# Declaring four ring slots of weights free together, behind the last value product of the mixing stage

## The reference, cut to what matters

```
xr, xw, xk, xv, xa, xg = [x + xx * mu[n] for n in range(6)]      # xx = x of the token before - x
r, k, v = xr @ w_rkv[0], xk @ w_rkv[1], xv @ w_rkv[2]            # 1024 x 1024 each
...
for each token t:                                                # state: 64 x 64 for each of 16 heads
    state = state * w_t + (state @ -kk_t) (kk_t * a_t) + v_t k_t
    y_t = state @ r_t
y = normalise(y) by head, times lnx_w, plus lnx_b, plus a bonus term times v
h = h + (y * g) @ w_o
```

## Time and profile before

| | |
|---|---|
| timed runs, us | 1700.23, 1700.84, 1712.27 (median 1700.84) |
| the profiled execution, us | 1709.79 |
| its span, first to last instruction, us | 1708.0 |
| mean granted TensorE clock | 0.988 of full speed |
| TensorE busy | 1667.2 us (98%) |
| the chain that ended last | TensorE 91%, VectorE 5%, DMA 2%, ScalarE 1% |

### The profile page before, as it was taken

How to read it: one execution, slowest core, us unless ns; L and a number is a source line. 1 busy time by engine, 2 the same in 40 slices (tenths; PEclk the granted TensorE clock), 3 DMA queues, 4 the chain that set the end, 5 groups by cost and what they waited for, 6 DMA issues and landing times.

```text
span 1708.0 us, 30174 instructions
## 1 busy us (share of the span) xinstructions
PE 1667.2 (98%) x12836; PEld 1297.3 (76%) x12836; DVE 906.1 (53%) x1926; ACT 699.5 (41%) x1348; POOL 5.0 (0%) x6
## 2 busy tenths in 40 slices
PE   9999999999999999999999999999989999999996
PEld 8889999787699699999887986555546798655553
DVE  6667565644467465657658765222126876523213
ACT  5576444432343354446548553111123655311111
POOL 0000000000000000000000000000000000000000
PEclk9999999999999999999999999999999999999998
DMA  8613353423200544525551455999992355599995
GB/s 338 246 70 146 156 221 125 169 99 148 88 3 4 221 184 162 214 108 197 195 187 38 175 194 217 426 424 424 425 423 82 110 196 198 218 427 426 422 426 225
DMA packets 36443, 373.80 MB, mean 219 GB/s; under 512 B 7232, under 2 KB 8384, under 8 KB 11728
## 3 DMA queue, kind: packets, MB, share of 16 engines
q1 hardware_dynamic: 33216, 366.18, 53.7%
q10 hardware_dynamic: 3088, 5.61, 1.0%
HBM read 370.73 MB, written 1.05 MB: 218 GB/s over the span
## 4 chain that ended last, share of the span: by engine, by line
PE 91%; DVE 5%; DMA 2%; ACT 1%; issue 1%; DVEq 0%; SPq 0%; ACTq 0%
PE ps L655 41%; PE ps L2346 12%; PE ps L2369 6%; PE ps L879 3%; PE ps L995 2%; PE ps L1526 2%; PE ps L2358 2%; PE ps L976 2%; PE ps L1770 2%; PE ps L2332 2%; PE ps L1739 2%; DMA ring<-in_w_moe 1%; PE ps L987 1%; PE ps L432 1%; PE ps L2834 1%; PE ps L2400 1%
## 5 line engine op out<-in xcount | busy, mean ns | idle before, releaser
L655 PE MATMUL ps<-ffn_x_h,ffn_w 128*128 128x256 f32 x1408 | 257.4, 283 | 0.2
L2346 PE MATMUL ps<-ring,expert_inputs 128*64 128x256 f32 x2048 | 235.1, 382 | 1.2 <-DMA ring<-in_w_moe 1.2
L655 PEld LDWEIGHTS ps<-ffn_x_h,ffn_w 128*128 128x128 f32 x1408 | 221.3, 192 | 1.5 <-DVE ffn_x_l L494 0.5
L647 ACT CAST w_h<-ring 128x512 fp32r<-128x512 f32 x240 | 149.3, 624 | 138.1 <-PE ps L655 130.0
L655 PE MATMUL ps<-ffn_x_l,ffn_w 128*128 128x256 f32 x704 | 199.2, 283 | 0.0
L650 DVE TENSOR_TENSOR w_l<-ring,w_h 128x512 fp32r<-128x512 f32 x240 | 164.1, 689 | 66.0 <-ACT w_h L647 62.0
L2346 PEld LDWEIGHTS ps<-ring,expert_inputs 128*64 128x64 f32 x2048 | 141.4, 137 | 70.4 <-DMA ring<-in_w_moe 1.3
L650 DVE TENSOR_TENSOR ffn_w<-ring,ffn_w 128x1024 fp32r<-128x1024 f32 x132 | 155.8, 1221 | 20.8 <-ACT ffn_w L647 20.8
L655 PE MATMUL ps<-w_h,x_h 128*128 128x512 f32 x384 | 150.1, 391 | 0.0
L655 PE MATMUL ps<-w_h,x_l 128*128 128x512 f32 x384 | 149.5, 389 | 0.0
L655 PE MATMUL ps<-w_l,x_h 128*128 128x512 f32 x384 | 149.4, 389 | 0.0
(11 more groups left out here) (374 smaller groups left out, 2674.6 us busy)
## 6 DMA issues: line engine op xcount, KB each, us to landing
ring<-in_w_moe SPq DMA_DIRECT2D x64, 2048.0 KB, 14.8
ring<-in_w_proj SPq DMA_DIRECT2D x37, 2048.0 KB, 8.0
ring<-in_w_ffn SPq DMA_DIRECT2D x22, 3072.0 KB, 10.2
ring<-in_w_moe SPq DMA_DIRECT2D x64, 1024.0 KB, 15.6
ring<-in_w_b_in SPq DMA_DIRECT2D x1, 2496.0 KB, 18.9
ring<-in_w_lora SPq DMA_DIRECT2D x1, 2048.0 KB, 8.1
rows<-in_ln_g SPq DMA_DIRECT2D x4, 512.0 KB, 3.6
rows<-in_ln_b SPq DMA_DIRECT2D x4, 512.0 KB, 5.1
```

The lines of the kernel that those rows point to most:

```text
L647: act.copy(high, x).then_inc(ready.up(), 1)
L655: last = pe.matmul(out, a[x], b[y], start=start and n == 0, stop=stop and n == 2, skip_group_check=True)
L2346: last = pe.matmul(bank(0)[g * SLOTS_E:(g + 1) * SLOTS_E, 0:2 * P], x[:, k, e * SLOTS_E:(e + 1) * SLOTS_E], wg[:, g, k, :], start=(k == 0) ...
```

## The change

Two lines are added behind the product of W6 on TensorE's list. `unit_done` issues nothing: it writes down, while the program is built, which semaphore value frees a slot. It is called a second time for W3, W4, W5 and W6 and overwrites what the calls inside `by_features` and `by_tokens` had set for them, one product at a time. The value is now that of the last product of W6, for all four.

```diff
                     last.then_inc(bonus_mm.up(), 1)
                     by_tokens(6, "v", V_OUT + 2)
+                    for i in range(3, 7):
+                        unit_done(j0 + i, mm)
                 stream(block, 6)
```

## The result

The changed kernel takes 1712.11 us (median of 20 runs, 1706.71 to 1722.24), the kernel before 1702.58 us (20 runs, 1699.62 to 1712.27). The ratio is 1.0055, with a 95% interval of 1.0041 to 1.0068: 9.4 us slower, 7.0 to 11.6. That is under the 1% that was named as the limit for a single comparison, but with this many runs it is clear of zero, and it is several times the 1.4 us that were forecast.

What follows compares the result with a forecast made beforehand. TensorE was taken to bound the kernel, with no transfer on the chain at the change. The only term, +1.4 us for VectorE's wait on the late lnx copies, added to the median gave 1702.2 us, range 1699.0 to 1709.0.

Steps and rivals of the forecast that it cites:

- What bounds the kernel: Whole kernel: TensorE busy 98% of the span, 91% of the chain; DMA 2%, no transfer on the chain at the change.
- what is moved: SP's loads wait for the end of W6's product: W7 later by 59.6 us, W8 by 42.4, W9 by 22.
- W7 to W9 themselves: The three loads in the scan: in by 485.2, first read at 552.01, 67 us of cover, so no cost.
- the products: Products ahead of the scan: loads leaving that stretch gain nothing, TensorE already busy throughout at clock 1.00; gain 0.
- What stands behind them in SP's queue: Four lnx copies queued behind W9: now behind 7 MB instead of 3, landing late for VectorE; the only cost seen.
- the sum: All terms together: +1.4 us with nothing against it, giving a median of 1702.2 us.
- The landing of the copies: Early scan: last lnx copy lands at 480.5 to 482.0, taken as 481.2.
- the wait that was priced at 1.4 us: First chunk: VectorE's copy of R starts at 481.2, but TensorE needs it by 479.8; cost 1.4 us, 0.7 to 2.2.
- The third rival: Scan: instruction fetches by DMA share engines with 7 MB; four fetches delayed 0.9 us each, 3.6 us, 1704.4; chance 0.05.
- The second rival: Around 482: the wait lowers TensorE's clock, +1.4 us; with slower loads, +2.8 to +8.2 us together; chance 0.15 including slower queue.
- The range: Median time of the changed kernel: 1699.0 to 1709.0 us, to hold the hidden case and most slower cases.
- The profile as a test: Signs of error: copies landing under 479.8, copies overtaking the loads, or granted clock 0.50 anywhere between 477 and 487.

Runs made afterwards that it cites:

- e8: Kernel before plus 6 MB of extra traffic beside the receptance and value products, where TensorE runs long matmuls; ratio 0.9994.
- e1: Changed kernel, but the four lnx copies issued ahead of W7, during the receptance products; ratio 1.0036 to the kernel before.
- e7: Kernel before, with only the four lnx copies (0.5 MB) held until the last value product; ratio 1.0003.
- e5: Kernel before, with W7, W8, W9 loaded a second time behind the last value product, 7 MB of extra traffic; ratio 1.0038.
- e3: Changed kernel, but W7, W8, W9 loaded in pieces of 4 KB per partition, all queued at once; ratio 1.0037 to the kernel before.
- e9: Changed kernel with lnx copies early and W7 to W9 in 0.5 MB pieces, each issued after the last landed; ratio 1.0002 to the kernel before.
- e11: Changed kernel with lnx copies early and W7 to W9 in 1 MB pieces, each issued after the last landed; ratio 1.0008 to the kernel before.
- e4: Changed kernel with lnx copies early and W7, W8, W9 issued 25 us apart in the scan; ratio 1.0043 to the kernel before.
- e6: Kernel before, with W7, W8, W9 loaded twice more behind the last value product, 14 MB of extra traffic; ratio 1.0072.
- e12: Changed kernel with lnx copies early and W7, W8, W9 as whole loads, each issued after the last landed; ratio 1.0037 to the kernel before.

## Why the prediction was wrong

**What bounds the kernel, what is moved, W7 to W9 themselves, the products**: right. TensorE carries the chain (92%), no load stands on it, W7 to W9 are in long before their use, and the products gained nothing by losing the loads (e8 adds some there without a loss).

**What stands behind them in SP's queue: "This is the one cost I see."** This is the step that failed, twice over: the cost was not there, and another, which the sum held at nothing ("+1.4 us, with nothing against it"), was. The landing of the copies was worked out to 0.3 us (24.3 forecast, 24.0 measured), from rows of queued loads. But the moment at which they are needed was taken from the trace of before, as if TensorE's work ahead of it stood fast under the new traffic. It didn't: the gaps and the low clock brought VectorE to its copy at 478.64 - 450.52 = 28.1 us into the scan, instead of 20.0. So the wait that was priced at 1.4 us was worth nothing: e1 takes it away and gains nothing at equal clock, e7 has the copies in the scan alone and loses nothing. In its place traffic alone costs 4.9 us at equal clock (e5), where the change costs 4.7.

**The third rival, "TensorE starves for instructions"**: it had the place, the condition and the sign, and got 0.05. What was wrong in it was its two numbers. It was priced at 0.9 us for a fetch, one 24 KB packet of wait, 3.6 us in all; the gaps were 2.25 and 3.25 us, and e3, with packets a quarter as long, had a gap of the same 2.25. The cost follows the queue (or how full the engines are), not the packet. And it was argued away by "none of the chain's time in the scan is put down to a fetch". That row was from a scan in which the DMA was idle: 0.02 of its engines' time in the 20 us after 457. A trace can't speak against a collision that it doesn't contain.

**The second rival, the clock**: its mechanism took place, but behind the gaps, not behind the wait on the copies. It was priced at 1.4 us for 3.5 us of low clock. In the profile the clock was 0.50 for at least the 12 us from 474 to 486. Over all runs it came to 2.8 us against the 35 runs of before and 4.4 against the 20; e1 and e5 show 1.4 and 2.3 against the runs of before beside them, so it varies from run to run.

**The sum.** 1.4 us forecast, 9.4 us measured, by the ratio; the means differ by 9.1 us (20 runs against 20 of before) or 7.5 (against the 35), of which 4.7 are at equal clock and the rest goes with the clock. The range ended at 1709.0. It was built on a median of three runs of before, 1700.84, 1.7 us under that of 20; the difference alone, 9.4, would have left it all the same.

**The profile as a test.** The prediction named "the granted clock is 0.50 anywhere between 477 and 487" as a sign that it was wrong, and this was the sign that came.

**Are the gaps late fetches of instructions?** The DMA records of the traces say so in four ways.

- The packets of kind instruction on queue q8 are 16 KB each, and from 450 to 560 one comes for every 250 to 259 matmuls and weight loads of TensorE, on average, in each of the 14 kernels. From 300 to 400 of the kernel before, where TensorE runs 5 matmuls a microsecond, there are 4 in 100 us. So their count goes with TensorE's instructions.
- They come late under the loads. In the dense part of the scan of before they start 3.7 us apart (465.02, 468.73, 472.46). In the changed kernel they start at 456.19, 462.18 and 469.43, thus 6.0 us apart the first time, though TensorE ran without a stop from 456 to 462.
- Work goes on behind each of them. In the changed kernel the two move from 462.18 to 463.13 and from 469.43 to 470.45, and the gaps end at 464.61 and 471.91, both 1.5 us later. All 22 gaps of the nine kernels that have any end 1.2 to 1.6 us behind the end of such a packet.
- The packet itself is not slow: from 450 to 560 it moves in 0.88 to 1.50 us in every kernel, 0.93 to 1.36 in the one before. The time is lost ahead of it.

The half microseconds from 462.0 and from 469.0 of the changed kernel have one each:

```profile
q8 instruction: 1, 0.02, 11.9%
...
q8 instruction: 1, 0.02, 12.8%
```

It fits that the gaps come only beside work that runs through instructions fast (e5 against e8), between matmuls that have no wait, and that they shrink when less is queued ahead (e9, e11). In e11 the packets start 4.7 to 5.2 us apart while the loads run.

**What stays open.** No trace says when a packet was asked for, so what holds it back is not shown: the depth of SP's queue, or how full the engines are. The Trainium skill, "DMA: Bandwidth & Descriptors", section "Queues, rings and completion order", says that each DMA engine takes turns between the queues, a whole packet at a time; by that a fetch would wait for one packet of the loads, at most. The runs don't bear it out for the packets that the trace counts: e3 and e9 have pieces of the same 4 KB, and only e3, with its deep queue, loses. By the page its packet holds several pieces; no trace here shows how many. Open too is why e4 lost more in its runs than its gaps account for.

## What to carry to other kernels

Before loads are moved, look at what the compute engine runs in the place they go to, not only at when they must be there: a stretch of short matmuls (here 64 x 64, some 35 a microsecond) is a bad host for a deep DMA queue, and a stretch of long ones a better one. If loads must go into such a stretch, issue them in pieces of half a megabyte, each behind the landing of the last: the same 7 MB then cost 0.4 us here, about the error, instead of 5. And read two profiled executions only together with the granted clock of many runs; here 0.001 of mean clock is 1.54 us, and the one pair of profiles hid three quarters of the loss.

There is no version here that beats both kernels; e9 and e8 come out even with the kernel before.

## What the runs showed of the hardware that was not expected

- TensorE halts for 0.3 to 3.3 us between matmuls that wait for nothing, while loads of 1 MB and more are under way or have just landed. The gap of 2.25 us came in four kernels (after, e3, e5, e6), to the hundredth.
- Each of the 22 gaps ends 1.2 to 1.6 us behind the end of a 16 KB instruction packet, and such a packet comes for every 250 to 259 of TensorE's matmuls and weight loads.
- The matmuls between the gaps are not slowed: in the full stretch from 456 to 462 TensorE began 207 of them at a clock of 1.00.
- After two halts of 2.25 and 3.25 us within 10 us the clock was at half (1.2 GHz) for 12 us at least, though TensorE was busy for 11.33 of these 12 us. In e12 one halt of 1.80 us was enough: the clock is 0.50 from 472 to 480.
- SP was held for 15.04 us in issuing two small copies behind 7 MB of loads, against 6.01 us behind 3 MB; with nothing ahead of them (e7) it was 1.32.
